# Eight of the twelve weight transfers of a lap are issued as four pairs with rows of 32 KB

## The reference

```python
def hierarchical_moe(x, w_group, b_group, w_router, b_router, w_gate, w_up, w_down):
    ...
    g_top_p, g_idx = lax.top_k(group_probs, 1)
    ...
    e_top_p, e_idx = lax.top_k(e_probs, TOP_K_IN_GROUP)
    ...
    combine = (group_onehot[:, :, None] * exp_w[:, None, :]).astype(x.dtype)
    y = jnp.zeros_like(xt)
    for g in range(N_GROUPS):
        h = jax.nn.silu(jnp.einsum('td,edf->tef', xt, w_gate[g])) * jnp.einsum('td,edf->tef', xt, w_up[g])
        y = y + jnp.einsum('tef,efd->td', h * combine[:, g, :, None], w_down[g])
    return y.reshape(B, S, D)
```

## Time and profile before

| what | us |
|---|---|
| three runs | 1118.16, 1118.86, 1120.52 (median 1118.86) |
| the profiled execution | 1117.6 |
| its span, first to last instruction | 1115.6 |
| TensorE busy | 905.4 (81%) |
| ScalarE, VectorE busy | 259.5, 136.3 |
| DMA | 433.77 MB, mean 389 GB/s |

### The profile page before, as it was taken

The page is one execution under the profiler, slowest core; times in us unless marked ns, Lnnn a source line. Parts: engine busy times, 40 slices in busy tenths (PEclk is TensorE's granted clock), DMA queues, the critical chain, the costliest instruction groups (busy, mean ns, idle before and its releaser), DMA issues.

```text
span 1115.6 us, 23639 instructions
## 1 busy us (share of the span) xinstructions
PE 905.4 (81%) x10138; PEld 556.7 (50%) x10138; DVE 136.3 (12%) x444; ACT 259.5 (23%) x577; POOL 17.9 (2%) x38
## 2 busy tenths in 40 slices
PE   8999999898868585868679998988877867685866
PEld 4788565554535352534345646555443434352533
DVE  1222330100000000000003523000000000000001
ACT  1165422322202020111102423122120202020201
POOL 0000000000000000000001100000000000000000
PEclk9999999999979999999999999999999999898988
DMA  9982369999999999999999946999999999999996
GB/s 365 428 363 88 115 260 404 430 427 429 428 428 430 427 429 428 429 429 428 429 427 426 424 180 224 428 428 428 430 427 429 428 429 428 428 430 428 429 429 278
DMA packets 31849, 433.77 MB, mean 389 GB/s; under 512 B 3536, under 2 KB 3792, under 8 KB 5584
## 3 DMA queue, kind: packets, MB, share of 16 engines
q1 hardware_dynamic: 31824, 433.42, 92.2%
HBM read 432.36 MB, written 1.05 MB: 388 GB/s over the span
## 4 chain that ended last, share of the span: by engine, by line
PE 46%; DMA 27%; SPq 20%; ACT 3%; DVE 2%; issue 2%; another core or an unknown queue 1%; DVEq 0%; POOLq 0%; ACTq 0%
DMA ring<-in_w_moe 26%; SPq L453 20%; PE ps L1319 10%; PE ps L1186 5%; PE ps L1371 5%; PE ps L1170 5%; PE ps L1111 3%; PE ps L1307 3%; PE ps L1294 3%; PE ps L1135 2%; PE ps L1395 2%; PE ps L1344 1%; PE ps L1362 1%; PE ps L1421 1%
## 5 line engine op out<-in xcount | busy, mean ns | idle before, releaser
L1319 PE MATMUL ps<-ring,xT 128*32 128x256 f32 x4096 | 272.5, 413 | 131.6 <-DMA ring<-in_w_moe 115.3
L1319 PEld LDWEIGHTS ps<-ring,xT 128*32 128x32 f32 x4096 | 131.5, 116 | 251.4 <-DMA ring<-in_w_moe 145.7
L1371 PE MATMUL ps<-ring,hT 128*32 128x256 f32 x2048 | 126.9, 389 | 33.7 <-DMA ring<-in_w_moe 22.8
L1371 PEld LDWEIGHTS ps<-ring,hT 128*32 128x32 f32 x2048 | 63.8, 111 | 79.7 <-issue 27.5
L673 ACT ACTIVATE sil<-ps 128x128 f32<-128x128 f32 x64 | 17.7, 277 | 357.3 <-PE ps L1319 357.3
L973 DVE TENSOR_TENSOR sil<-sil,ps 128x128 f32<-128x128 f32 x64 | 18.4, 288 | 601.9 <-ACT sil L673 601.9
L1294 PE MATMUL ps<-oT 32*128 32x256 f32 x1024 | 76.6, 415 | 8.1 <-ACT oT L678 8.1
L1111 PE MATMUL ps<-par 128*128 128x256 f32 x288 | 75.0, 396 | 5.9 <-ACT hT L676 5.9
L1307 PE MATMUL ps<-oT,h 128*128 128x128 f32 x512 | 74.1, 288 | 1.0 <-DVE oT L958 0.7
L1307 PEld LDWEIGHTS ps<-oT,h 128*128 128x128 f32 x512 | 61.9, 190 | 19.1 <-issue 11.2
L1294 PEld LDWEIGHTS ps<-oT 32*128 32x128 f32 x1024 | 48.4, 193 | 41.1 <-issue 23.3
(11 more groups left out here) (149 smaller groups left out, 560.0 us busy)
## 6 DMA issues: line engine op xcount, KB each, us to landing
ring<-in_w_moe SPq DMA_DIRECT2D x192, 2048.0 KB, 48.7
ring<-in_w_a SPq DMA_DIRECT2D x7, 2048.0 KB, 29.5
ring<-in_w_b SPq DMA_DIRECT2D x4, 2048.0 KB, 42.7
ring<-in_w_a SPq DMA_DIRECT2D x2, 512.0 KB, 5.6
ring<-in_w_a SPq DMA_DIRECT2D x1, 1024.0 KB, 9.1
h<-in_x SPq DMA_DIRECT2D x2, 512.0 KB, 14.3
ring<-in_w_b SPq DMA_DIRECT2D x1, 1024.0 KB, 44.2
out<-h SPq DMA_DIRECT2D x4, 256.0 KB, 2.1
```

What stands on the lines that cost most here:

```text
L1319: last = MM(ps[CAP * j:CAP * (j + 1), B_GU, 0:2 * P].rearrange("p (u f) -> p u f", u=2), xg[:, kk, CAP * e:CAP * (e + 1)], w[:, :, k, P * ...
L1371: last = MM(ps[CAP * c:CAP * (c + 1), B_Y, 0:256], hT[:, b, CAP * j:CAP * (j + 1)], w[:, j, 256 * c:256 * (c + 1)], start=j == 0, stop=j = ...
```

## The change

The slots of a lap are grouped by a new list, `LOADS`: slots 1 and 2 alone, then 3 and 4, 5 and 6, 7 and 8, 9 and 10 together, then 11 and 12 alone (the list counts them from 0). A pair is one transfer of 4 MiB: 128 rows of 32 KB in device memory, to two buffers that lie side by side in every partition. In `MOE_AT` both slots of each such pair do have neighbouring buffers, in both layers, so that the order is kept. `expert_slots` lays out the weights of a lap so that the two slots of a pair alternate row by row.

SyncE waits for a pair until its second buffer is free (`s + n` in the place of `s + 1`). A pair raises only the `landed` of its first buffer, by 16, and TensorE's `wait_m` for either slot of the pair waits on that one (`SIGNAL`). All other transfers, the order of TensorE's work and `free_quad` stay.

```diff
+LOADS = [(0, 1), (1, 1), (2, 2), (4, 2), (6, 2), (8, 2), (10, 1), (11, 1)]
...
-    return np.concatenate([both, last], 2).reshape(3 * EXP, P, SLOT)
+    laps = np.concatenate([both, last], 2).reshape(NQ, SLOTS_QUAD, P, SLOT)
+    return np.concatenate([laps[:, s:s + n].transpose(0, 2, 1, 3).reshape(NQ, -1) for s, n in LOADS], 1)
...
-        PER = [[MOE_AT[l].count(b) for b in range(RING)] for l in range(2)]
+
+        SIGNAL = [[MOE_AT[l][s0] for s0, n in LOADS for _ in range(n)] for l in range(2)]
+        PER = [[int(b in SIGNAL[l]) for b in range(RING)] for l in range(2)]
...
-            b = MOE_AT[layer][s]
-            here = 16 * (IN_A[b] + layer * IN_B[b] + MOE_AT[layer][0:s].count(b) + 1)
+            b = SIGNAL[layer][s]
+            here = 16 * (IN_A[b] + layer * IN_B[b] + 1)
...
-                    for s in range(SLOTS_QUAD):
-                        src = w_moe[layer][bass.ds(g * SLOTS_QUAD + s, 1)].rearrange("a p n -> (a p) n")
-                        load(MOE_AT[layer][s], src, its, layer * RING + s + 1)
+                    lap = w_moe[layer][bass.ds(g, 1)]
+                    for s, n in LOADS:
+                        b = MOE_AT[layer][s]
+                        src = lap[:, P * SLOT * s:P * SLOT * (s + n)].rearrange("a (p n) -> (a p) n", p=P)
+                        sp_.wait_ge(freed, its * SLOTS_QUAD + (layer * RING + s + n))
+                        sp_.dma_start(ring[:, b:b + n, :].rearrange("p b n -> p (b n)"), src
+                                      ).then_inc(landed[b], 16)
```

## The result

The changed kernel takes 1126.76 us (median of 5 runs, 1125.09 to 1127.35) against 1118.86: a ratio of 1.0064, with a 95% interval of 1.0050 to 1.0078. In microseconds this is +7.2 (5.6 to 8.7). The forecast was +4.7, the range went to 1128.5. The profiled execution took 1126.76 us with a span of 1124.4, 8.8 us more than that of before.

What follows compares the result with a forecast made beforehand. The prediction took the kernel as a serial sum of attention, weight streams and the work left after their last landings. Rows -3.5, issue 0, landing +5.6 and clock +2.6 gave +4.7 us, 1123.6 us; range 1119.8 to 1128.5.

Steps and rivals of the forecast that it cites:

- What bounds the kernel: Whole kernel: serial sum of attention, the weight streams of laps 2 to 8, and TensorE work after each layer's last landing.
- Part 1, longer rows: Streams of both layers: rows of 32 KB instead of 16 KB gain 3.5 us over 56 pairs; bounds 0 and -3.9.
- rival (b): Streams: rows of 32 KB are moved as pieces of 16, so nothing is saved; +8.2, 1127.1 us; chance 0.12.
- (d): Streams: longer rows are read more slowly, +3.5 in place of -3.5; +11.7, 1130.6 us; chance 0.04.
- Part 2, issue: Stream starts: a pair issued only when its second buffer is free lands no later; 0, bounds -1 and +1 per layer.
- Part 3, landing: Layer ends: slot 9 waits for slot 10, leaving a 12.71 us TensorE chain behind it; +2.78 each, together +5.6.
- Part 4, the clock: Layer ends: TensorE's clock falls after longer gaps, slowing the chain's head; 1.3 us each, +2.6; bounds 0 and 2.65 each.
- the prediction's +5: Clock loss at the layer ends if, as the skill says, both pay: nearer the upper bound, at +5 us.
- Sum: Whole kernel: -3.5 + 0 + 5.6 + 2.6 = +4.7 us; 1123.6 on the scale of the median.
- Rival (a): Layer ends: clock holds or falls elsewhere, rows save all of 3.7; +1.9 to 2.2, no difference; chance 0.17.
- (c): Streams: the change of transfer, not the row, holds the engines; faster, 1117.2 or 1115.2 us; chance 0.07.

Runs made afterwards that it cites:

- the filled gap: Changed kernel with 8 products that nobody reads added ahead of the wait for slot 9 in each lap; measured 1.0049, +5.5 us against before.

## Why the prediction was right, and where not

**What bounds the kernel** held: a serial sum of streams and what is left behind them. Starts, streams and ends, added up from the one trace of each kernel, come within 1.1 us of the measured change in eight of the eleven kernels; they are 1.6 too low for the one with the last pair undone, 2.1 too low for the filled gap, and 1.6 too high for all pairs without keep-warm products.

**Part 1, longer rows:** -3.5 was put, -4.0 is what the two streams show, at the bound of -3.9. The streams of the kernels with three, two and one pair a lap gained less in proportion (1.5 and 1.3 us, 1.0 and 1.0, 0.4 and 0.5), and those with rows of 16 KB nothing. Rows of 32 KB go as one packet, so rival (b) is out, and so is (d). The pair saves 0.07 us, about 9 ns for each row that falls away (8 per engine), against 8.2 from the rows of 4 KB. The Trainium skill ("DMA: Bandwidth & Descriptors", section "Why small descriptors are slow") gives a packet 3 cycles, 3.5 ns at its 850 MHz, and besides, which the prediction left out, 32 bytes of descriptor; by an estimate from 26.8 GB/s an engine (428.5 / 16) these are 1.2 ns more. By an estimate from these figures the streams would have gained 1.5 us over their 54 pairs, or 2.0 with the descriptors; the trace has 4.0, so they are too few for this kernel. What that page of the Trainium skill has on rows over 64 KiB, which the prediction puts under "Queues, rings", stands in its section "Why a DMA increments its semaphore by 16 and not by 1".

**Part 2, issue: here is the step that failed.** It let the pair land 9.7 us behind slot 2, at the full rate from its first row on. The issue was early enough, as it said (177.82, 4.5 us ahead of slot 2's landing at 182.32), but the landing came 10.97 us behind slot 2's, and 10.69 in layer 1: at 193.3, where this gave 189.6 + 1.7 (the later start of the whole) = 191.3. 0 was put, with bounds of +1 for each layer. The starts came 2.3 us later in the profiled execution, past the bounds, of which 1.3 lie behind slot 2, where the pair can act; over all traces the pair costs 1.0 + 1.3 us there. The ratios give 4.6 (3.1 to 5.9) in the kernel with that pair alone, and nothing that can be told between the two kernels without keep-warm products. That the cost exists is shown by the traces and by the kernel with a pair only there; its size in one kernel or another, and why the first rows are slow, is open.

**Part 3, landing:** the chain of 12.71 us, +2.78 at each end. The filled gap shows the chain by itself (12.7 us from the third to the fourth down at both ends), the kernels with and without the last pair that this pair makes the loss at the ends, and the one without keep-warm products that the length of the chain is the cause. The last down of before did not quite wait for its own landing, as the prediction puts it: it carries no bracket in the earlier trace rows and starts 0.28 us after slot 12 had landed, at the end of the work behind slot 11. That work had hardly any slack left even then.

**Part 4, the clock:** 1.3 per end was put; the third down took 1.60 and 1.55 us longer, at a granted clock of 0.51 and 0.50. In the trace of after TensorE waited for a slot for over 4.5 us 12 times, and each time the 32 products behind the wait ran at the low level, wholly or for the greater part; before had no wait over 3.0 us, and behind 25 of its 48 waits of over 1.5 us they ran at the high level throughout. By the Trainium skill ("TensorE: Matmul & The Clock Gate", section "HAM oscillation") work shorter than its wait starts cold each time, and both ends were to pay. Both did, though the work ahead of the wait was slightly longer than the wait (4.99 against 4.81 us); but they did not pay the prediction's +5, since the rest of the chain ran at the high level. The expected fall of the mean clock below 0.9 was too much: it went to 0.91.

**Sum:** -4.0 + 2.3 + 5.6 + 3.1 = +7.0 against +4.7; of the 2.3 us between them 2.3 are the starts, +0.5 the clock and -0.5 the rows. The sign, the place and the largest term were right, and the measured +7.2 lies inside the range, toward its upper end. The time alone would have spoken for rival (b), whose 1127.1 is nearer to 1126.76 than the forecast's 1123.6; only the packets and the rate put (b) out. That +7.0 and +7.2 agree so well is in part luck: the 1.0 us of the starts that is slot 2's own differs from execution to execution. Rival (a) fell with the clock, (c) with the pairs of 16 KB rows: fewer transfers alone gain nothing.

## What to carry to other kernels

A larger transfer gains by its rows all along a stream and is paid for at the stream's two ends, where its last part holds up its first: count the work that is chained behind the last landings and in front of the first issue, and leave small what stands there. Here the edit is +0.64% with all four pairs, +0.71% with the last alone and -0.23% with the two middle ones. And products that keep an engine warm are free only as long as the engine waits there anyway: once the wait moved ahead of them, 9 of them became 4.5 us of critical path in each layer. Taking them out shortened the two ends by 4.5 and 3.6 us and turned the change from +7.2 to -3.6 us.

## What the runs showed of the hardware

- SyncE can be held in its issue itself. Before, a transfer's issue took 0.33 us when few were queued, but 3.55 in the median and up to 12.6, and SyncE waited for a free buffer once in 840 to 1050 us (0.6 us). After, no issue takes over 0.35 us, and it is the buffers that hold SyncE back, 28 times in that stretch. With pairs of 16 KB rows, the same number of transfers and bytes, issues take up to 8.2 us: so what fills depends on the number of rows, not on that of bytes or transfers. The issues of the weights (ns, min/median/max), of before, of after, and of the pairs with rows of 16 KB:

```profile
L453 SPq DMA_DIRECT2D ring<-in_w_moe x192: 332/3548/12602, 17.3 to 1053.0; - x192
```

```profile
L483 SPq DMA_DIRECT2D ring<-in_w_moe x128: 332/333/347, 17.4 to 1057.0; - x128
```

```profile
L481 SPq DMA_DIRECT2D ring<-in_w_moe x128: 333/378/8220, 18.6 to 1061.4; - x128
```

- A row as such costs one of the 16 engines about 9 ns, still to be seen at 16 KB (0.07 us a pair, over 8 rows). The completions cost nothing that shows in the rate: 853 and 544 of them in the same 260 us, both at 428 GB/s with rows of 16 KB.
- In the changed kernel the first transfer of 4 MiB of a stream moves its first rows below the rate that it reaches later, with the engines busy all the time (DMA share 0.97 and 0.96): 382 and 367 GB/s over 7 us, then 429 and 434.
- The first 10 us come in two lengths, 1 to 2 us apart, whatever the kernel: the first products of the first projection run at half speed in some executions and at full speed in others, one (with slots 1 and 2 paired) lying between. A difference of 2 us between two single executions of this kernel says nothing.
